# Two feed-forward stages: gate and up products as seven products of quarters, gated values and residual through DRAM, down projection after them

## Chip, cores and metric

The kernel runs on one core of one Trainium2 chip. The metric is the time of one execution on the device in microseconds (us), as the median of several runs. The profile of one execution stands beside it.

## What is computed

Two transformer blocks act on 1024 tokens of width 1024, all in float32, the second on the result of the first. Each has a mixer (attention of several kinds), then a feed-forward part with 2816 hidden features, and it is only this part that the change rewrites:

```python
def hybrid_layer(...):
    ...
    gu = jnp.einsum('bsd,df->bsf', x, w_gu)
    gate, up = gu[..., :FFN_HIDDEN], gu[..., FFN_HIDDEN:]
    ffn = jnp.einsum('bsf,fd->bsd', jax.nn.silu(gate) * up, w_down)
    return layer_norm(DEEPNORM_ALPHA * x + ffn, ln2_g, ln2_b)

def second_block(...):
    ...
    f = (jax.nn.silu(h @ w_gate[l]) * (h @ w_up[l])) @ w_down[l]
    x = x + gate_f * rmsnorm(f, g_ffn_post[l])
```

## The kernel before

**Products.** A float32 product is made of three float32r products. Each operand is split into a high part (rounded to float32r) and a low part (what is left), and TensorE adds high x high, low x high and high x low in one PSUM bank: the lines L444 to L446 (`pe_gemm_f`, features on the bank's partitions) and L469 to L471 (`pe_gemm_t`, tokens on the partitions). All move 512 columns against a 128 x 128 weight block.

**Weights.** A list `plan` names all weight tiles of 512 KB in the order of their use. SyncE loads them into three buffers `raw` (`sp_feed`, L405). ScalarE copies a tile to the high part `wh` (`act_feed`, L416), GpSimd subtracts to get the low part `wl` (`pool_feed`, L425); of each part there are five buffers (`NU = 5`). `ahead(m)` works out how many loads and splits may be issued once unit m is used. In layer 1, tiles of `w_cond_2` ("R" units, the modulation rows of the second block) go through the same three buffers, and VectorE uses them up in `dve_mod` (L1568, L1571).

**Feed-forward part.** The normalised tokens stand transposed and split in `yh`, `yl`. The 22 blocks of 128 hidden features are taken in chunks of 6, 6, 6 and 4. For each feature block and each half of the tokens (512), gate and up take 24 matmuls each. ScalarE takes silu of the gate bank (L1674), VectorE multiplies by the up bank (L1733), ScalarE writes the high part (L1693) and VectorE the low part (L1737) into `hh`, `hl`, which stay in SBUF. After each chunk the down projection of its features is made for 8 blocks of tokens x 2 halves of columns, and VectorE adds each bank into `res` (L1753), which in layer 1 holds the residual, scaled by ScalarE (L1496). Five banks take turns in all of this.

**Order.** Each engine's program is written by hand (`pe_ffn`, `act_ffn`, `pool_ffn`, `dve_ffn`, `sp_ffn`) and run strictly in order; engines wait for each other by semaphores alone. All DMAs are issued from SyncE's queue.

Of the kernel before, what the change touches and what calls it, by code (L numbers as in the profile page):

```python
# [9 lines left out]
F32 = mybir.dt.float32  # L10
# [162 lines left out]
def build(nc, T, out):  # L173
    with ExitStack() as top:
# [37 lines left out]
        x3_out, y_out = sem("x3_stored"), sem("out_stored")  # L212
        xb_in = [sem(f"xb_in{i}") for i in range(4)]
# [58 lines left out]
        def ffn_memory(name):  # L272
            area(upper)
            sil = [sb(f"sil{i}" + name, 512) for i in range(2)]
            hh, hl = [sb("hh" + name, 4096, FR)], [sb("hl" + name, 4096, FR)]
            spare = place[0]
            hh.append(sb("hi" + name, 2048, FR))
            hl.append(sb("hm" + name, 2048, FR))
            return sil, hh, hl, spare

        sil1, hh1, hl1, spare = ffn_memory("_gu")
        macc = [sb(f"macc{i}", 512) for i in range(2)]
        area(spare)
# [14 lines left out]
        sil2, hh2, hl2, spare = ffn_memory("_gate")  # L298

# [19 lines left out]
        ROWS = 6, 5  # L319

        def has_row(a, k, f):
            return a < 18 and f < a + k - 1
# [12 lines left out]
        m = 0  # L335
        for a, k in CHUNKS:
            for f in range(a, a + k):
                plan += [("F", "w_gu", 128 * f), ("F", "w_gu", FF + 128 * f)]
                if has_row(a, k, f):
                    plan += mod_rows(m, 1)  # L340
                    m += 1
            for n in range(2):
                plan += [("T", "w_down", j, 512 * n) for j in range(a // 2, (a + k) // 2)]
                if a < 18:
                    plan += mod_rows(m, ROWS[n])
                    m += ROWS[n]
# [4 lines left out]
        for a, k in CHUNKS:  # L351
            for f in range(a, a + k):
                plan += [("F", "w_gate_2", 128 * f), ("F", "w_up_2", 128 * f)]
            for n in range(2):
                plan += [("T", "w_down_2", j, 512 * n) for j in range(a // 2, (a + k) // 2)]
        unit = {key: m for m, key in enumerate(plan)}
        split_units = [m for m, key in enumerate(plan) if key[0] != "R"]
        split_no = {m: n for n, m in enumerate(split_units)}

        room = {}  # L360

        def ahead(m):

            if m not in room:
# [2185 lines left out]
```

## Time and profile before

| | us |
|---|---|
| median of 3 runs | 2666.53 |
| lowest, highest | 2664.0, 2666.94 |
| the profiled execution | 2664.65 |
| its span | 2662.5 |
| TensorE busy | 2509.5 (94%) |
| VectorE, ScalarE, GpSimd busy | 1144.1, 843.2, 494.5 |
| mean granted TensorE clock | 0.976 of full |
| moved by DMA | 205.44 MB |

The span reaches from the first to the last instruction; what lies around it in the profiled execution is 2664.65 - 2662.5 = 2.15 us. Line numbers (L444) are those of the kernel's file. A matmul's duration in the profile overlaps the next one's, so TensorE's pace is read from the count of matmuls in a stretch and not from their durations.

### The profile page before, as it was taken

How to read it: one execution, taken by the hardware profiler on the slowest of the kernel's cores; microseconds unless marked ns; L12 is line 12 of the kernel's file. 1: busy time of each engine (PE TensorE's matmuls, PEld its weight loads, DVE VectorE, ACT ScalarE, POOL GpSimd, SP SyncE). 2: the span in 40 equal slices, each digit the busy share in tenths (PEclk: the TensorE clock that was granted, in tenths of full speed). 3: DMA queues.
4: the chain of work that ended last, by engine and by line, in shares of the span. 5: the costliest groups of instructions: out<-in, count | busy, mean ns of one | idle time of the engine just before them, and what ended most of it. 6: DMA issues, size and time to landing. Idle time of an engine off the chain costs nothing.

```text
span 2662.5 us, 31098 instructions
## 1 busy us (share of the span) xinstructions
PE 2509.5 (94%) x12551; PEld 2032.0 (76%) x12551; DVE 1144.1 (43%) x2177; ACT 843.2 (32%) x1532; POOL 494.5 (19%) x209
## 2 busy tenths in 40 slices
PE   7999988879999999999999989989899999999998
PEld 6667877668877787787787866667778888888886
DVE  2698897753623223223319037773631111111115
ACT  3556637651311111121123226653421112021112
POOL 2012210001122122222223211021212222222220
PEclk9999988989999999999999999989999999999999
DMA  5015441222033323323412210001411111111122
GB/s 157 16 52 183 161 151 54 101 82 106 8 95 103 95 71 95 96 70 97 151 51 78 78 40 25 17 17 64 135 64 48 40 56 48 52 46 53 57 70 103
DMA packets 195718, 205.44 MB, mean 77 GB/s; under 512 B 13788, under 2 KB 143340, under 8 KB 195576
## 3 DMA queue, kind: packets, MB, share of 16 engines
q1 hardware_dynamic: 195576, 203.46, 24.4%
q8 instruction: 99, 1.62, 0.3%
q14 instruction: 43, 0.35, 0.0%
HBM read 170.88 MB, written 32.56 MB: 76 GB/s over the span
## 4 chain that ended last, share of the span: by engine, by line
PE 77%; DVE 15%; ACT 3%; issue 2%; DMA 2%; POOL 1%; SPq 1%; POOLq 0%; DVEq 0%; ACTq 0%
PE bank L444 15%; PE bank L446 15%; PE bank L445 15%; PE bank L469 8%; PE bank L471 8%; PE bank L470 8%; DVE rest L2136 2%; PE bank L1306 2%; DVE junk L1021 2%; DVE res L1241 1%; POOL wl L425 1%; PE bank L1216 1%; DVE took L2141 1%; PE bank L488 1%; PE bank L1280 1%
## 5 line engine op out<-in xcount | busy, mean ns | idle before, releaser
L425 POOL TENSOR_TENSOR wl<-raw,wh 128x1024 fp32r<-128x1024 f32 x189 | 455.4, 2428 | 2037.9 <-ACT wh L416 2037.9
L444 PE MATMUL bank<-yh,wh 128*128 128x512 f32 x1536 | 602.9, 393 | 5.7 <-ACT sil_gu L1674 2.8
L445 PE MATMUL bank<-yl,wh 128*128 128x512 f32 x1536 | 599.3, 390 | 0.0
L446 PE MATMUL bank<-yh,wl 128*128 128x512 f32 x1536 | 599.3, 390 | 0.0
L416 ACT ACTIVATE wh<-raw 128x1024 fp32r<-128x1024 f32 x189 | 196.1, 1054 | 546.4 <-PE bank L471 242.9
L444 PEld LDWEIGHTS bank<-yh,wh 128*128 128x128 f32 x1536 | 289.7, 189 | 71.9 <-issue 5.4
L446 PEld LDWEIGHTS bank<-yh,wl 128*128 128x128 f32 x1536 | 289.3, 188 | 60.5
L445 PEld LDWEIGHTS bank<-yl,wh 128*128 128x128 f32 x1536 | 289.5, 189 | 59.5 <-issue 0.2
L1733 DVE TENSOR_TENSOR sil_gate<-sil_gate,bank 128x512 f32<-128x512 f32 x44 | 30.3, 688 | 358.9 <-PE bank L446 358.6
L1733 DVE TENSOR_TENSOR sil_gu<-sil_gu,bank 128x512 f32<-128x512 f32 x44 | 30.2, 687 | 324.9 <-PE bank L446 212.0
L1753 DVE TENSOR_TENSOR res<-bank,res 128x512 f32<-128x512 f32 x112 | 76.0, 689 | 214.0 <-PE bank L471 214.0
L469 PE MATMUL bank<-wh,yh 128*128 128x512 f32 x384 | 151.5, 395 | 2.7 <-DVE yl L2153 1.5
L470 PE MATMUL bank<-wl,yh 128*128 128x512 f32 x384 | 149.9, 390 | 0.0
L471 PE MATMUL bank<-wh,yl 128*128 128x512 f32 x384 | 149.8, 390 | 0.0
L1021 DVE TENSOR_SCALAR_CACHE_REDUCE junk<-score,cand 128x384 bf16<-128x384 f32 (+3 forms) x132 | 108.9, 825 | 4.7
L444 PE MATMUL bank<-xh,wh 128*128 128x512 f32 x240 | 96.6, 402 | 6.3 <-POOL wl L425 6.3
L469 PE MATMUL bank<-wh,hh_gu 128*128 128x512 f32 x256 | 100.6, 393 | 1.0 <-POOL wl L425 1.0
L469 PE MATMUL bank<-wh,hh_gate 128*128 128x512 f32 x256 | 99.7, 389 | 1.0 <-POOL wl L425 1.0
L471 PE MATMUL bank<-wh,hl_gu 128*128 128x512 f32 x256 | 99.7, 389 | 0.0
L470 PE MATMUL bank<-wl,hh_gu 128*128 128x512 f32 x256 | 99.6, 389 | 0.0
L471 PE MATMUL bank<-wh,hl_gate 128*128 128x512 f32 x256 | 99.6, 389 | 0.0
L470 PE MATMUL bank<-wl,hh_gate 128*128 128x512 f32 x256 | 99.6, 389 | 0.0
(287 smaller groups left out, 4092.2 us busy)
## 6 DMA issues: line engine op xcount, KB each, us to landing
raw<-in_w_cond SPq DMA_DIRECT2D x48, 512.0 KB, 3.9
raw<-in_w_gu SPq DMA_DIRECT2D x44, 512.0 KB, 5.3
raw<-in_w_down SPq DMA_DIRECT2D x44, 512.0 KB, 3.6
raw<-in_w_in SPq DMA_DIRECT2D x40, 512.0 KB, 4.1
raw<-in_w_gate SPq DMA_DIRECT2D x22, 512.0 KB, 3.9
raw<-in_w_up SPq DMA_DIRECT2D x22, 512.0 KB, 3.9
res<-in_x SPq DMA_DIRECT2D x16, 512.0 KB, 8.4
raw<-in_w_out SPq DMA_DIRECT2D x16, 512.0 KB, 3.6
```

Source lines behind the costliest of these rows:

```text
L416: act.i.activation(wh[n % NU][:, :], raw[u % NRAW][:, :], ACT.Copy).then_inc(*av.up(("wh", u)))
L425: pool.i.tensor_tensor(wl[n % NU][:, :], raw[u % NRAW][:, :], wh[n % NU][:, :].bitcast(F32), ALU.subtract).then_inc(*po.up(("wl", u)))
L444: pe.i.matmul(bank[:, :], a, a_h[:, s], start=k == 0, stop=False)
L445: pe.i.matmul(bank[:, :], a, a_l[:, s], start=False, stop=False)
L446: last = pe.i.matmul(bank[:, :], b, a_h[:, s], start=False, stop=k == 7)
L469: pe.i.matmul(bank[:, 0:wide], xa, h[:, c:c + wide], start=k == 0, stop=False)
L470: pe.i.matmul(bank[:, 0:wide], xa, l[:, c:c + wide], start=False, stop=False)
L471: last = pe.i.matmul(bank[:, 0:wide], xb_, h[:, c:c + wide], start=False, stop=k == nk - 1)
L1021: dve.i.tensor_scalar(junk[:, 0:ln], score[:, o:o + ln], 0.0 if thr is None else thr[:, n:n + 1], 0.0, op, ALU.add, accum_out=cnt[:, n:n + ...
L1306: last = pe.i.matmul(uses.held[t, "out"][:, c0:c1], pt[:, 128 * b:128 * b + 128], v[:, 128 * b + c0:128 * b + c1], start=b == 0, stop=b == i)
L1733: dve.i.tensor_tensor(sil[:, :], sil[:, :], uses.held[key][:, :], ALU.mult).then_inc(*dv.frees(uses, key))
L1753: dve.i.tensor_tensor(dst, uses.held[key][:, :], dst, ALU.add).then_inc(*dv.frees(uses, key))
```

## The change

**Seven products.** The first four feature blocks ("early") of each layer are made as before, 24 matmuls a bank. The other 18 are taken two at a time, gate and up apart: 18 "pairs" q per layer, even q gate, odd q up. A pair is a product of 1024 tokens x 1024 inputs with 256 features. The inputs are cut into quarters (512 tokens x 512 inputs), the weights too (512 inputs x 128 features), and the four quarters of the result are combined from seven products of quarters, in the Winograd form of Strassen's scheme. A product has 4 blocks of inputs x 3 = 12 matmuls, a pair 84 where it had 96.

**Sums of tokens.** Four sums of token quarters are made once per layer while the early features run: VectorE in pieces of 128 x 2048 (`dve_sum`), ScalarE the high part (`act_sum`), VectorE the low part (`dve_sum_low`). `sum1` takes the place of a quarter of `yh`, `yl` that the early features read.

**Differences of weights.** Four differences of 128 x 512 per pair are made by VectorE from the two raw tiles into `res` (`wdiff`, `dve_feed`). The split into high and low is made in pieces of 128 x 512, two to a unit "S".

**Putting together.** ScalarE copies product 0 to SBUF; VectorE makes seven additions with a bank per pair (`dve_pair`); on even pairs ScalarE takes four silus in place, on odd pairs VectorE makes four multiplications.

**Hidden values through DRAM.** Gated values are stored in `qk_d` (22 blocks of 512 KB), read back, and split by ScalarE and VectorE in pieces of 128 x 1024 (`sp_hidden`, `act_hidden`, `dve_hidden`): blocks 0 to 5 beside the last pair, later ones beside the down projection, which is now a stage of its own after all pairs, in the same chunks and with as many matmuls.

**Residual.** In layer 1 the normalised tokens are stored in `x2_d` (`sp_out1`) and read back (`sp_residual`) before the down projection; VectorE scales them in its first addition, and the eight scaling copies of ScalarE (L1496) go.

**Modulation rows.** One row per pair and 5 + 5 per chunk (before 5 in a chunk's features and 6 + 5 in its down part); 48 as before.

```diff
@@ def ffn_plan(layer, m) @@
+            for q in range(N_PAIR):
+                f = N_EARLY + q // 2 * 2
+                units += [("W", wu if q % 2 else wg, (up if q % 2 else 0) + 128 * (f + i)) for i in range(2)]
+                if layer == 1:
+                    units += mod_rows(m, 1)
+                    m += 1
+                units += [("S", layer, i) for i in range((7 * q) // 2, (7 * q + 7) // 2)]
...
+        def operands(u):
+            layer, i = plan[u][1:]
+            out = []
+            for o in (2 * i, 2 * i + 1):
+                b1, b2 = [raw_of(w) for w in pair_units(layer, o // 7)]
+                out.append(((b1[:, 0:512], b1[:, 512:1024], wdiff[1], wdiff[2], wdiff[0], wdiff[3], b2[:, 512:1024])[o % 7],
...
+        def dve_feed(m):
...
+                dve.i.tensor_tensor(t1, b12, b11, ALU.subtract).then_inc(*dv.up())
+                dve.i.tensor_tensor(t3, b22, b12, ALU.subtract).then_inc(*dv.up())
+                dve.wait_ge(*dv.now())
+                dve.i.tensor_tensor(t2, b22, t1, ALU.subtract).then_inc(*dv.up())
+                dve.wait_ge(*dv.now())
+                dve.i.tensor_tensor(t4, b21, t2, ALU.subtract).then_inc(*dv.up(("differences", layer, q)))
...
+                if plan[u][0] == "S":
+                    for k, (src, there) in enumerate(operands(u)):
+                        act.wait_ge(*there)
+                        act.i.activation(wh[n % NU][:, 512 * k:512 * k + 512], src, ACT.Copy).then_inc(*av.up(("wh", u)))
...
+        PRODUCTS = a11, a12, sum2, sum3, sum1, a22, sum4
+        SUM_OF = {2: 2, 3: 3, 4: 1, 6: 4}
...
+        BESIDE_LAST = {1: (0, 1), 3: (2, 3), 5: (4, 5)}
...
+        def pe_pair(layer, q):
+            for s, (high, low) in enumerate(PRODUCTS):
...
+                h, l = pe_unit(u)
+                bank = G["r"].open(key)
+                pe.wait_ge(*G["r"].prior(key))
+                if q == 0 and s in SUM_OF:
+                    pe.wait_ge(*dv.after(("sum_low", layer, SUM_OF[s])))
+                for k in range(4):
+                    c = 512 * (o % 2) + 128 * k
+                    pe.i.matmul(bank[:, :], h[:, c:c + 128], high[:, k, :], start=k == 0, stop=False)
+                    pe.i.matmul(bank[:, :], h[:, c:c + 128], low[:, k, :], start=False, stop=False)
+                    last = pe.i.matmul(bank[:, :], l[:, c:c + 128], high[:, k, :], start=False, stop=k == 3)
...
+        def sp_hidden(layer, f):
+            to, i = landing(f)
...
+            elif f < 6:
+                sp.wait_ge(*dv.after(("landed", layer, f - 2)))
...
+            sp.i.dma_start(to, T["qk_d"][f].rearrange("p (k c) -> p k c", k=2)).then_inc(*hid_in[i].up((layer, f), 16))
...
+        def act_pair(layer, q, s):
+            if s == 0:
...
+                act.i.activation(first[q % 2], uses.held[key][:, :], ACT.Copy).then_inc(*av.frees(uses, key))
+            elif s in ENDS and q % 2 == 0:
+                p = piece(q, *ENDS[s])
+                act.wait_ge(*dv.after(("done", layer, q, s)))
+                act.i.activation(p, p, ACT.Silu).then_inc(*av.up(("gated", layer, q, s)))
...
+                    if not n and not tb:
+                        pe.wait_ge(*dv.after(("landed", layer, a + kk - 1)))
```

**What moves on the engines, by the built programs.** TensorE has 9737 rows where it had 10169: 432 matmuls fewer. The first place is VectorE inside layer 1's pairs. Before, one feature block with its modulation row (`macc`) reads:

```order
L1733 TENSOR_TENSOR sil0_gu_122<-sil0_gu_122,bank0 128x512
L1737 TENSOR_TENSOR hl_gu_125<-sil0_gu_122,hh_gu_124 128x512
L1733 TENSOR_TENSOR sil1_gu_123<-sil1_gu_123,bank2 128x512
L1737 TENSOR_TENSOR hl_gu_125<-sil1_gu_123,hh_gu_124 128x512
L1571 SCALAR_TENSOR_TENSOR macc0_128<-raw2_56,cc_51,macc0_128 128x512 x2
```

Now, at the seam from an odd pair to the even one behind it (the last rows of the odd pair, the differences for the pair after, its row, its first additions):

```order
L1995 TENSOR_TENSOR res_53<-bank4,res_53 128x512
L2002 TENSOR_TENSOR res_53<-res_53 128x512
L477 TENSOR_TENSOR res_53<-raw0_54,raw2_56 128x512
L478 TENSOR_TENSOR res_53<-raw0_54 128x512
L480 TENSOR_TENSOR res_53<-raw0_54,res_53 128x512
L482 TENSOR_TENSOR res_53<-raw2_56,res_53 128x512
L1659 TENSOR_SCALAR macc1_131<-raw1_55,cc_51 128x512
L1662 SCALAR_TENSOR_TENSOR macc1_131<-raw1_55,cc_51,macc1_131 128x512
L1995 TENSOR_TENSOR res_53<-bank1,res_53 128x512
L2006 TENSOR_TENSOR res_53<-bank2,res_53 128x512
```

The differences stand in front of the additions that free the banks, so VectorE waits there for both raw tiles of the next pair. The second place is SyncE's queue in layer 1's pairs. Before, each feature block has this:

```order
L405 DMA raw0_54<-in_w_cond_2 128x2x512 [waits dve_done]
L405 DMA raw1_55<-in_w_gu 128x8x128 [waits pool_done,act_done]
L405 DMA raw2_56<-in_w_gu 128x8x128 [waits pool_done,act_done]
```

Now two pairs have this:

```order
L447 DMA raw1_55<-in_w_cond_2 128x2x512 [waits dve_done]
L447 DMA raw2_56<-in_w_gu 128x8x128 [waits pool_done,act_done]
L447 DMA raw0_54<-in_w_gu 128x8x128 [waits pool_done,act_done]
L2111 DMA qk_d<-res_53 128x1024 [waits dve_done] x2
L447 DMA raw1_55<-in_w_cond_2 128x2x512 [waits dve_done]
L447 DMA raw2_56<-in_w_gu 128x8x128 [waits pool_done,act_done]
L447 DMA raw0_54<-in_w_gu 128x8x128
```

In one pair of two the second tile waits for splits that need the first tile's arrival; in the other both are issued together. Two stores have come in. The third place is SyncE's queue at the end of layer 2's pairs. Before, a chunk's features and its down projection follow on each other with loads of weights alone:

```order
L405 DMA raw2_56<-in_w_gate_2 128x8x128 [waits pool_done,act_done]
L405 DMA raw0_54<-in_w_up_2 128x8x128 [waits pool_done,act_done]
L405 DMA raw1_55<-in_w_gate_2 128x8x128 [waits pool_done,act_done]
L405 DMA raw2_56<-in_w_up_2 128x8x128 [waits pool_done,act_done]
L405 DMA raw0_54<-in_w_down_2 128x2x512 [waits pool_done,act_done]
```

Now:

```order
L1807 DMA res_53<-qk_d 128x1024 [waits early_stored1,early_stored0] x2
L447 DMA raw0_54<-in_w_down_2 128x2x512 [waits pool_done,act_done]
L1807 DMA res_53<-qk_d 128x1024 [waits early_stored1,early_stored0,dve_done] x2
L447 DMA raw1_55<-in_w_down_2 128x2x512 [waits pool_done,act_done]
L1807 DMA res_53<-qk_d 128x1024 [waits hid_stored2,dve_done]
L1807 DMA res_53<-qk_d 128x1024 [waits hid_stored3,dve_done]
```

The six hidden blocks that the first chunk of the down projection needs come in three turns through two landing places, and each of the last four waits for VectorE to have split the block two before it.

## Rows read from the trace of the kernel before

**Rows 1.** Page, busy time by engine; then TensorE clock in 40 slices.

```profile
PE 2509.5 (94%) x12551; PEld 2032.0 (76%) x12551; DVE 1144.1 (43%) x2177; ACT 843.2 (32%) x1532; POOL 494.5 (19%) x209
...
PEclk9999988989999999999999999989999999999999
```

**Rows 2.** Page, chain that ended last, by engine.

```profile
PE 77%; DVE 15%; ACT 3%; issue 2%; DMA 2%; POOL 1%; SPq 1%; POOLq 0%; DVEq 0%; ACTq 0%
```

**Rows 3.** Busy us (x instructions) by stretch, core 0; first line names columns.

```profile
core 0: us, PE busy (x) PEld busy (x) DVE busy (x) ACT busy (x) POOL busy (x), PEclk, DMA share, GB/s
690.00:1440.00 750.00, 743.10 (x3262) 602.54 (x3261) 249.83 (x334) 143.01 (x195) 171.50 (x72) 1.00 0.29 87
...
1940.00:2620.00 680.00, 675.52 (x2976) 559.05 (x2975) 108.64 (x156) 121.50 (x161) 145.16 (x62) 0.99 0.17 52
2100.00:2200.00 100.00, 100.00 (x443) 82.84 (x442) 13.51 (x20) 16.86 (x22) 21.83 (x10) 1.00 0.17 48
```

**Rows 4.** What PE waited for, 690 to 1430 us: total, times, longest.

```profile
PE bank L444 <- ACT sil_gu L1674: 2.8, 1, 2.8
```

**Rows 5.** Groups, 690 to 1430 us: count, busy, mean ns, idle before.

```profile
L425 POOL TENSOR_TENSOR wl<-raw,wh 128x1024 fp32r<-128x1024 f32 x66 | 157.9, 2411 | 588.7 <-ACT wh L416 588.7
...
L1571 DVE SCALAR_TENSOR_TENSOR macc<-raw,cc,macc 128x512 f32<-128x512 f32 x84 | 73.6, 877 | 5.4
L416 ACT ACTIVATE wh<-raw 128x1024 fp32r<-128x1024 f32 x65 | 68.4, 1059 | 313.4 <-DMA raw<-in_w_gu 185.4 <-DMA raw<-in_w_down 107.6 <-PE bank L471 20.3
...
L1737 DVE TENSOR_TENSOR hl_gu<-sil_gu,hh_gu 128x512 fp32r<-128x512 f32 x32 | 31.8, 993 | 22.4 <-ACT hh_gu L1693 22.4
L1733 DVE TENSOR_TENSOR sil_gu<-sil_gu,bank 128x512 f32<-128x512 f32 x44 | 30.2, 687 | 324.9 <-PE bank L446 212.0 <-ACT sil_gu L1674 112.9
...
L1693 ACT ACTIVATE hh_gu<-sil_gu 128x512 fp32r<-128x512 f32 x32 | 20.2, 632 | 136.4 <-DVE sil_gu L1733 136.4
...
L551 DVE SCALAR_TENSOR_TENSOR res<-res,st,b 128x1024 f32<-128x1024 f32 x6 | 7.7, 1284 | 0.2
```

**Rows 6.** GpSimd's two forms of one operation, whole span.

```profile
L688 POOL TENSOR_TENSOR wil<-wir,wih 128x64 fp32r<-128x64 f32 x1 | 0.3, 324 | 4.7 <-ACT wih L677 4.7
```

**Rows 7.** ScalarE in time, 725 to 760 us.

```profile
739.49 1.06 ACT L416 ACTIVATE wh<-raw 128x1024 fp32r<-128x1024 f32 x1 [8.57 <-DMA raw<-in_w_gu]
...
742.12 0.58 ACT L1674 ACTIVATE sil_gu<-bank 128x512 f32<-128x512 f32 x1
```

**Rows 8.** TensorE in time, 736 to 744 us: the gap.

```profile
743.15 0.47 PE L444 MATMUL bank<-yh,wh 128*128 128x512 f32 x1 [2.81 <-ACT sil_gu L1674]
743.45 0.39 PE L445 MATMUL bank<-yl,wh 128*128 128x512 f32 x1
```

**Rows 9.** Loads into raw, 700 to 800 us: issue to landing.

```profile
DMA to landing us min/median/max: 3.8/5.3/7.9
```

**Rows 10.** Page, a DMA issue line: count, KB each, median us to landing.

```profile
raw<-in_w_gate SPq DMA_DIRECT2D x22, 512.0 KB, 3.9
```

**Rows 11.** VectorE in time, 790 to 830 us.

```profile
820.88 0.69 DVE L1733 TENSOR_TENSOR sil_gu<-sil_gu,bank 128x512 f32<-128x512 f32 x1 [8.80 <-PE bank L446]
822.26 2.60 DVE L1737 TENSOR_TENSOR hm_gu<-sil_gu,hi_gu 128x512 fp32r<-128x512 f32 x1 [0.70 <-ACT hi_gu L1693]
```

**Rows 12.** GpSimd in time, same stretch: three instructions end to end.

```profile
817.20 7.12 POOL L425 TENSOR_TENSOR wl<-raw,wh 128x1024 fp32r<-128x1024 f32 x3 [13.92 <-ACT wh L416]
```

**Rows 13.** TensorE in time, 1944 to 1947 us.

```profile
1943.95 1.97 PE L488 MATMUL bank<-con,xb 128*128 128x128 f32 x8 [3.48 <-DVE xb L2308]
...
1946.57 0.63 PE L446 MATMUL bank<-yh,wl 128*128 128x512 f32 x1
```

**Rows 14.** Windows with the columns of rows 3: clock is third from last.

```profile
1944.00:1948.00 4.00, 4.00 (x14) 3.52 (x15) 3.71 (x5) 2.81 (x5) 0.00 (x0) 0.50 0.88 359
1948.00:1952.00 4.00, 4.00 (x16) 3.17 (x15) 1.55 (x3) 1.09 (x2) 0.00 (x0) 0.79 0.00 0
```

More of the change, by code:

```diff
@@ L270, in build @@
         g1, b1 = sb("g1", 1024), sb("b1", 1024)
[L272 to L281, printed above, removed]
+        area(upper)
+        sums = {n: [sb(f"sum{n}{x}", 2048, FR) for x in "hl"] for n in (2, 3, 4)}
+        early = [sb(f"early{i}", 512) for i in range(2)]
         macc = [sb(f"macc{i}", 512) for i in range(2)]
+        wdiff = [res[:, 512 * i:512 * i + 512] for i in range(4)]
+        first, third, whole = [res[:, 2048:2560], res[:, 2560:3072]], res[:, 3072:3584], res[:, 3584:4096]
+        hid = [res[:, 4096:6144], res[:, 6144:8192]]
+        spare = upper + 9216
         area(spare)
@@ L406, in sp_feed @@
                 fed["sp"] += 1
+        def operands(u):
[4 more added lines that the diff above has]
+                out.append(((b1[:, 0:512], b1[:, 512:1024], wdiff[1], wdiff[2], wdiff[0], wdiff[3], b2[:, 512:1024])[o % 7],
+                            loaded(pair_units(layer, o // 7)[o % 7 > 1]) if o % 7 in (0, 1, 6) else dv.after(("differences", layer, o // 7))))
+            return out
@@ new lines, in next_hidden, with blocks_of, hidden_store, piece @@
+        def next_hidden(a, n, tb):
+            i = 8 * n + tb
+            last = min(a + 12, 22)
+            return a + 6 + i // 2 if a < 18 and i % 2 and a + 6 + i // 2 < last else None
+        BESIDE_LAST = {1: (0, 1), 3: (2, 3), 5: (4, 5)}
+        def blocks_of(q):
+            f = N_EARLY + q // 2 * 2
+            return f, hid[(f // 2 + 1) % 2]
+        def hidden_store(f):
+            return 2 * ((f // 2 + 1) % 2) + f % 2
+        def piece(q, block, half):
+            c = 1024 * block + 512 * half
+            return blocks_of(q)[1][:, c:c + 512]
@@ L1718, in pool_ffn, with dve_pair @@
                         after_block(tb)
+        def dve_pair(layer, q, s):
+            if s == 0:
+                return
+            key = ("product", layer, q, s)
+            bank, u, f = uses.held[key], first[q % 2], blocks_of(q)[0]
+            dve.wait_ge(*mm.after(key))
+            dve.wait_ge(*dv.now())
+            if s in ENDS:
+                to = whole
+                if q % 2 == 0:
+                    to = piece(q, *ENDS[s])
+                    for i in range(2):
+                        dve.wait_ge(*hid_out[hidden_store(f + i)].after((layer, f + i - 4)))
+                if s == 1:
+                    dve.wait_ge(*av.after(("product", layer, q, 0)))
+                dve.i.tensor_tensor(to, bank[:, :], third if s in (4, 5) else u, ALU.add
+                                    ).then_inc(*(dv.up() if s == 4 else dv.frees(uses, key)))
+                dv.also(("done", layer, q, s))
+                if q % 2:
+                    p = piece(q, *ENDS[s])
+                    dve.wait_ge(*av.after(("gated", layer, q - 1, s)))
+                    dve.wait_ge(*dv.now())
+                    dve.i.tensor_tensor(p, whole, p, ALU.mult).then_inc(*dv.up(("hidden", layer, q, s)))
+            if s == 3:
+                dve.i.tensor_tensor(third, bank[:, :], u, ALU.add).then_inc(*dv.frees(uses, key))
+            elif s in (2, 4):
+                dve.i.tensor_tensor(u, bank[:, :], u, ALU.add).then_inc(*dv.frees(uses, key))
```

518 lines of the change are left out of this document (363 added, 155 removed).

## The prediction

> **What bounds the kernel now.** I read the page first. TensorE is busy for 94% of the span at nearly full clock, no other engine for half of it [rows 1], and the chain of waits that ended last lies on TensorE for 77% [rows 2]. Then the table by stretch: both feed-forward stages, 690 to 1440 us and 1940 to 2620 us, are TensorE without gaps, 743.10 of 750 and 675.52 of 680 us, while VectorE has 249.83 and 108.64 us of work there and GpSimd 171.50 and 145.16 [rows 3]. In layer 1 TensorE waited for another engine's result hardly at all; the one long wait is 2.8 us [rows 4]. So a matmul taken out here is worth its whole pace, as long as the other engines keep up. That pace is read from a stretch with nothing else in it: 443 matmuls in 100 us, 0.2257 us each [rows 3].
>
> **What goes.** Per layer 18 pairs with 84 matmuls instead of 96, so 2 x 18 x 12 = 432, as the built programs also show (10169 rows, now 9737). 432 x 0.2257 = **97.5 us**. The down projection and the early features keep their matmuls. A product now takes 12 x 0.2257 = 2.71 us, a pair 19.0 us. The 2.8 us wait comes from a bank whose silu stood behind ScalarE's splits, which waited for late loads [rows 4, 7, 8]; those loads were held up by the modulation row in front of them, and since the first features run in another order now and the next loads have another place, I take this wait as gone: 2.8 us. The scaling copies of ScalarE are off TensorE's path and count nothing either way.
>
> **What comes, engine by engine.** The work of a pair of 19.0 us in layer 1:
> - VectorE: 4 differences, 7 additions, 2 multiplications (4 in every second pair), 2 row updates. A 128 x 512 operation takes 0.69 us [rows 5, 11], a row update 0.88 us [rows 5]: 13 x 0.69 + 1.8 = 10.8 us.
> - ScalarE: 7 half splits at 0.63, a copy at 0.6, on average 2 silus at 0.58 [rows 5, 7]: 6.2 us.
> - GpSimd: 7 half subtractions. No row has 128 x 512. Between 0.32 us for 64 columns [rows 6] and 2.41 us for 1024 [rows 5] a straight line gives 1.3 us, the upper bound is 2.41 (as if a half cost as much as a whole). I take 1.3, since 64 columns cost so little: 9.1 us; at the bound it would be 16.9 us, still under 19.0.
> - DMA: 22 stores and 22 loads of 512 KB more per layer and the residual there and back, on DMA engines that are busy for 29% and 17% of these stretches [rows 3]; the weights are as many as before.
>
> None of them is the bound by its sum. What can cost is order. Four places:
>
> *1. The start of layer 1's pairs.* The sums run on VectorE beside the early features (4 x 96 x 0.2257 = 87 us). A piece of 128 x 2048 isn't in the trace; from 0.69 us for 512 and 1.28 for 1024 columns [rows 5] I extend to 2.4 us (bounds 1.28 and 2.8). Fourteen of them are 34 us, covered. But `sum1` may be written only when the last early product has ended, and product 4 of pair 0 needs it 4 x 2.71 = 10.8 us later. In between lie, in layer 1, the second raw tile of pair 1 (its buffer comes free late, 4 to 5 us), four differences (2.8), ScalarE's half split and high part (0.6 + 1.9, extended in the same way) and VectorE's low part (2.4): 12 to 13 us. With a lock or two as in case 2, I take 3 us lost, with 0 and 8 as ends. In layer 2 the buffers have no modulation rows in them and the tile is early: 0.
>
> *2. Raw buffers in layer 1's pairs.* The three buffers hold two tiles of a pair and a modulation row, and the next tile may come only when the last piece of the old one is split. Over two pairs the chain is: load 3.9 (one alone [rows 9, 10]), ScalarE and GpSimd half 1.9, load 3.9, differences 2.8, half split 0.6, row update with first addition and silu 2.8 and split 1.3, four GpSimd halves 5.2; then two loads together 5.2, differences 2.8, half split 0.6, four halves 5.2. Sum 36.2 us, against 2 x 19.0 = 37.9 us of matmuls (unrounded). To this comes a wait that the trace shows: a VectorE operation with both inputs in SBUF took 2.60 us instead of 0.69 [rows 11], because GpSimd was at work from 817.20 for 7.12 us, three instructions end to end [rows 12], and VectorE's result came 0.54 us after these had ended. The operation just before, with one input in PSUM, took 0.69. GpSimd will be busy for 9.1 of 19.0 us, so each of some ten such operations in the chain waits 0.48 x 0.65 = 0.3 us on average: 3.1 us. The chain is then 39.3 us, 1.4 us longer than the matmuls, nine times in layer 1: 12.6 us, of which the splits that run ten products ahead hide some 8. I take **5 us**, between 0 and 33. In layer 2 two tiles share three buffers and the same chain is near 28 us: 0.
>
> *3. From the pairs to the down projection, both layers.* Counted from the start of the last pair, TensorE is done at 19.0. Hidden blocks 0 and 1 are loaded by then, but their places are free only after product 1, at 5.4. ScalarE takes 1.06 [rows 5], VectorE 1.28 (its one form of 1024 columns in the stage, L551) [rows 5]: block 0 split at 7.8, block 1 at 9.4. Each turn from there is a load (3.9 alone [rows 10], 4.1 with another behind it), 1.06 and 1.28, so 6.4 us: block 3 at 15.8, block 5 at 22.2, and with 1.3 us for the waits of case 2, 23.5. TensorE waits 4.5 us. After such a gap its clock is low: when it had waited 3.48 us [rows 13] the granted clock was 0.50 for the next 4 us, its level of 1.2 GHz, and 0.79 in the 4 us after [rows 14], and a matmul lasted 0.63 us [rows 13]; but after the 2.81 us gap the next one had 0.39 at once, as everywhere at full clock [rows 8]. Some 5 us at half pace lose about 2 us; I take these. Together 6.5 us per layer, **13 us**; ends 0 and 22.
>
> *4. Layer 1's first chunk.* The residual's last blocks, hidden blocks 6 to 9 and modulation rows queue behind the store of block 21. VectorE then frees its first bank some 3 us late and stands at hidden block 6 until about 15 us into the chunk; five banks of 4.1 us cover that. The last weight tile of the second half is there about when it is needed. I take 1 us, ends 0 and 6.
>
> **The sum.** 2664.65 - 97.5 - 2.8 + 3 + 5 + 13 + 1 = 2586.4 us for the profiled execution. That one lies 1.9 us under the median of 2666.53, so as a median **2588 us**, 2.9% faster.
>
> **A rule against this change.** The rows show that VectorE waited for GpSimd, once. The Trainium skill ("SBUF — State Buffer", Who interferes with whom) is stricter: GpSimd and a VectorE instruction with two SBUF inputs hold the shared port pair for a whole instruction, and the other one "fully blocks". The change puts six to eight such instructions into each pair and cuts GpSimd's work into pieces, so by that rule nearly every one may meet a lock; what that would give is the fourth case below. For the sums the skill has a figure too ("GPSIMD Engine Reference", Elementwise side-by-side cycle accounting): 2293 ns for 128 x 2048 on VectorE, which would take 0.1 us off each piece and leave the sum as it is.
>
> **Cases.**
> - *Forecast, 0.48:* 2575 to 2600 us.
> - *All covered, 0.15:* loads land in 3.8 us and the hidden blocks make it: 2666.5 - 97.5 - 2.8 + 2 = 2568 us. For it: TensorE hardly waited in either stage before [rows 4]. Against it: three turns of 6.4 us don't fit into 13.6 us.
> - *Layer 1's raw buffers become the bound, 0.30:* loads of w_gu take 5.3 us in the median and up to 7.9 [rows 9], and ScalarE stood 8.57 us before one [rows 7]. With 1.4 us more for each of three load steps the chain is 39.3 + 4.2 = 43.5 us, 5.6 more than the matmuls, nine times: 50 - 8 = 42 instead of 5, so 2625 us; half of the excess gives 2604. Against it: these 5.3 us are of loads issued three at a time, and the same kind alone lands in 3.9 [rows 10].
> - *Slower than before, 0.04:* the shared port locks at every meeting. Place: layer 1's chain of case 2. Ten VectorE operations wait a whole 1.3 us each instead of 0.3 and GpSimd halves cost 2.41 instead of 1.3 (nine of them in the chain): 43.5 + 10 + 10 = 63.5 us, 25.6 over, nine times 230 - 8: 2588 - 5 + 222 = 2805 us. It decides from the point where the chain passes 37.9 + (2666.5 - 2588 + 5 + 8) / 9 = 48 us. Against it: 9.1 of 19.0 us is GpSimd's share, not all.
> - *Something that I can't place, 0.03,* of either sign.
>
> That the change doesn't do what it says is excluded by the count of rows.
>
> **Range and chances.** A measurement of this kernel tells about 0.2% (5.3 us) from no change. 2569 us takes in most of the second case, 2622 us most of the third. Faster 0.95, within 0.2% 0.01, slower 0.04.
>
> **What will show it.** The stage of layer 1 is shorter by about 36 us (48.8 + 2.8 - 3 - 5 - 6.5 - 1) and that of layer 2 by 42 (48.8 - 6.5). TensorE's waits show one of 4 to 5 us before the first matmul of the down projection, for VectorE's low part of block 5, with a granted clock near 0.5 behind it in both layers; one of a few us for VectorE's `yl` at product 4 of layer 1's first pair; and in layer 1's pairs few or none. If the pairs of layer 1 take over 19.5 us and those of layer 2 19.0, the raw buffers bind. GpSimd's 128 x 512 pieces near 1.3 us, VectorE's differences at 0.69 with some up to 2.0. I am wrong if layer 2's pairs have waits, if TensorE's pace in a product isn't 0.2257 us, or if the early features take more than 87 us.

## Result and profile after: 2619.28 us

| | before | after |
|---|---|---|
| median | 2666.61 (4 runs) | 2619.28 (4 runs, 2619.0 to 2620.41) |
| the profiled execution | 2664.65 | 2619.53 |
| its span | 2662.5 | 2617.4 |

The ratio is 0.9825 (95% 0.9808 to 0.9842): 47 us, or 1.8%, faster, where 78 us were forecast. The time lies inside the range, near its slow end.

The page's busy time and granted clock by slice, and the chain of waits by engine, against [rows 1, 2]:

```profile
PE 2427.5 (93%) x12119; PEld 1959.3 (75%) x12119; DVE 1517.2 (58%) x2557; ACT 931.6 (36%) x1704; POOL 677.5 (26%) x389
...
PEclk9999988889999999999999999998989999999999
...
PE 61%; DVE 19%; DMA 7%; POOL 5%; ACT 4%; issue 3%; SPq 1%; DVEq 0%; POOLq 0%; ACTq 0%
```

TensorE has 432 matmuls fewer and is still the busiest. But the chain now lies on it for 61% and no longer for 77%; DMA has come to 7% of it and GpSimd to 5%. Where, a table by stretch tells (columns of [rows 3]): the stage of layer 1 with the start of the next mixer, layer 1's 18 pairs, and those of layer 2.

```profile
691.62:1531.57 839.95, 797.84 (x3453) 642.41 (x3451) 465.97 (x573) 209.56 (x328) 289.30 (x173) 0.98 0.36 120
782.20:1157.10 374.90, 358.23 (x1521) 289.30 (x1519) 219.67 (x269) 104.44 (x180) 168.64 (x121) 0.97 0.34 108
2013.00:2356.00 343.00, 342.94 (x1513) 283.62 (x1512) 178.80 (x231) 109.62 (x181) 164.55 (x122) 1.00 0.29 91
```

The first stretch, from the first early product to the first matmul of the next mixer, was this long before:

```profile
692.96:1538.15 845.19, 833.71 (x3669) 676.67 (x3667) 279.46 (x383) 169.23 (x243) 196.16 (x83) 1.00 0.29 86
```

So layer 1 gained 5.2 us where 36 were forecast. Layer 2's stage begins 4.8 us ahead (1939.17 against 1943.95 us) and ends 45.1 ahead: 40.3 gained where 42 were forecast. In layer 2's pairs TensorE works without a gap, 19.05 us each, as predicted; in layer 1 the same 18 pairs take 32 us more (4 of them are the modulation rows' own short matmuls, which the prediction's 19.0 us per pair left out: without a wait these pairs take 347.4 us, e1 below). Here is what TensorE waited for, 690 to 1445 us, where [rows 4] had one wait:

```profile
PE bank L1855 <- ACT res L1916: 16.4, 6, 4.5
PE bank L558 <- DVE res L2063: 11.0, 4, 7.9
PE bank L558 <- DVE sum3l L1820: 6.7, 1, 6.7
...
PE bank L1855 <- DVE yl L1768: 0.2, 1, 0.2
```

Three places, then: inside the pairs (16.4 us), at the handover to the down projection (6.7), and in the last chunk of the down projection (11.0). The last row is the wait for `sum1`, for which 3 us had been set aside. In layer 2, 1935 to 2610 us, the handover comes again:

```profile
PE bank L558 <- DVE sum3l L1820: 6.4, 1, 6.4
```

**One stall in the pairs**, 861 to 878 us in time (start, duration, instruction, idle before):

```profile
861.85 7.68 SPq L447 DMA_DIRECT2D raw<-in_w_gu  x2
...
865.78 1.16 ACT L495 ACTIVATE wh<-raw 128x512 fp32r<-128x512 f32 x2 [8.11 <-DMA raw<-in_w_gu]
866.55 2.54 POOL L510 TENSOR_TENSOR wl<-raw,wh 128x512 fp32r<-128x512 f32 x2 [4.78 <-ACT wh L495]
...
873.79 0.69 DVE L477 TENSOR_TENSOR res<-raw,raw 128x512 f32<-128x512 f32 x1 [9.53 <-DMA raw<-in_w_gu]
...
876.57 0.63 ACT L495 ACTIVATE wh<-res 128x512 fp32r<-128x512 f32 x1 [9.63 <-DVE res L482]
...
877.11 0.58 ACT L1916 ACTIVATE res<-bank 128x512 f32<-128x512 f32 x1
```

SyncE issues the first tile of the next pair at 861.85 us. It lands 3.9 us later; ScalarE makes two high halves, GpSimd two low halves, done at 869.09. Only then is the second tile issued (the two issues, 7.68 us with the wait between them, end at 869.53), and it lands at 873.8. VectorE's four differences and ScalarE's half split stand in front of the copy of product 0 (L1916), and that copy frees the bank for which TensorE waits:

```profile
877.74 0.79 PE L1855 MATMUL bank<-yh,wh 128*128 128x512 f32 x1 [4.49 <-ACT res L1916]
878.33 0.63 PE L1856 MATMUL bank<-yl,wh 128*128 128x512 f32 x1
```

Matmuls then stand 0.43 us apart instead of 0.2267 until 883.8 us, for 6 us, at the lower of the two clocks, 1.2 GHz: the granted clock (third from last) was 0.50 behind this wait and 0.51 behind the one at layer 2's handover.

```profile
877.70:881.70 4.00, 3.96 (x9) 3.13 (x10) 3.39 (x6) 3.16 (x6) 3.80 (x4) 0.50 0.43 135
2362.30:2368.70 6.40, 6.36 (x15) 5.00 (x16) 2.64 (x2) 0.00 (x0) 2.22 (x1) 0.51 0.44 143
```

How long is the chain over two pairs? The first of the four differences is made 17 times in layer 1's pairs, so from the first to the last there are eight periods of two pairs. Line L477, 780 to 1165 us:

```profile
L477 DVE TENSOR_TENSOR res<-raw,raw x17: 691/693/1687, 785.2 to 1125.7; 128x512 f32<-128x512 f32 x17
...
  DMA raw<-in_w_gu: 94.1, 14
```

(1125.7 - 785.2) / 8 = **42.6 us**, and before 14 of the 17 VectorE stood idle for a tile, 94 us in all. Predicted were 39.3.

**The last chunk of layer 1.** VectorE before the change and after it:

```profile
1314.85 0.21 DVE L1596 TENSOR_TENSOR macc<-macc 128x48 f32<-128x48 f32 x1 [10.44 <-DMA macc<-in_b_cond]
1324.79 1.23 DVE L1802 SCALAR_TENSOR_TENSOR gp<-sh,gp 128x1024 f32<-128x1024 f32 x1 [9.73 <-DMA sh<-vec_d]
```

```profile
1381.17 0.21 DVE L1687 TENSOR_TENSOR macc<-macc 128x48 f32<-128x48 f32 x1 [9.26 <-DMA macc<-in_b_cond]
1391.04 1.23 DVE L2153 SCALAR_TENSOR_TENSOR gp<-sh,gp 128x1024 f32<-128x1024 f32 x1 [9.66 <-DMA sh<-vec_d]
1392.18 1.28 DVE L2063 TENSOR_TENSOR res<-bank,res 128x512 f32<-128x512 f32 x2
```

The same two waits of VectorE, 19 to 20 us, stood there before. TensorE then had four feature blocks in front of it (4 x 96 x 0.2257 = 87 us) whose first banks it needed back late; now the chunk is down projection alone, a bank fills in 2.7 us, five are full after 13.6, and TensorE stands for 7.9 us.

### The profile page after: what moved, and what is told of

Its sections match the earlier page's. It is cut to its first block, busy times and chain, and to the rows that moved or that the text cites. A ratio compares the mean times of both kernels' runs of the same rounds, so it can differ in the third digit from the quotient of the medians.

```text
span 2617.4 us, 31377 instructions
## 1 busy us (share of the span) xinstructions
PE 2427.5 (93%) x12119; PEld 1959.3 (75%) x12119; DVE 1517.2 (58%) x2557; ACT 931.6 (36%) x1704; POOL 677.5 (26%) x389
## 4 chain that ended last, share of the span: by engine, by line
PE 61%; DVE 19%; DMA 7%; POOL 5%; ACT 4%; issue 3%; SPq 1%; DVEq 0%; POOLq 0%; ACTq 0%
PE bank L558 8%; PE bank L560 8%; PE bank L559 8%; PE bank L534 5%; PE bank L535 5%; PE bank L536 5%; PE bank L1855 5%; PE bank L1857 5%; PE bank L1856 5%; DMA raw<-in_w_gu 4%; POOL wl L510 4%; DVE rest L2487 2%; PE bank L1395 2%; DVE junk L1110 2%; DVE res L1330 1%
## 5 line engine op out<-in xcount | busy, mean ns | idle before, releaser
L515 POOL TENSOR_TENSOR wl<-raw,wh 128x1024 fp32r<-128x1024 f32 x117 | 294.0, 2527 | 1390.0 <-ACT wh L498 1390.0
L558 PE MATMUL bank<-wh,yh 128*128 128x512 f32 x768 | 303.7, 395 | 28.0 <-DVE sum3l L1820 13.1
L560 PE MATMUL bank<-wh,yl 128*128 128x512 f32 x768 | 300.5, 391 | 0.0
L1855 PE MATMUL bank<-yh,wh 128*128 128x512 f32 x576 | 228.6, 397 | 16.7 <-ACT res L1916 16.4
L510 POOL TENSOR_TENSOR wl<-raw,wh 128x512 fp32r<-128x512 f32 x108 | 155.1, 1450 | 283.0 <-ACT wh L495 283.0
L1857 PE MATMUL bank<-yh,wl 128*128 128x512 f32 x576 | 227.2, 395 | 0.0
L1856 PE MATMUL bank<-yl,wh 128*128 128x512 f32 x576 | 227.2, 394 | 0.0
L510 POOL TENSOR_TENSOR wl<-res,wh 128x512 fp32r<-128x512 f32 x144 | 191.3, 1351 | 119.5 <-ACT wh L495 99.2
L534 PE MATMUL bank<-yh,wh 128*128 128x512 f32 x384 | 154.0, 401 | 2.9 <-DVE ql L2383 1.4
L535 PE MATMUL bank<-yl,wh 128*128 128x512 f32 x384 | 151.1, 393 | 0.0
L536 PE MATMUL bank<-yh,wl 128*128 128x512 f32 x384 | 150.9, 393 | 0.0
L1855 PEld LDWEIGHTS bank<-yh,wh 128*128 128x128 f32 x576 | 109.8, 191 | 45.7 <-ACT res L1916 19.0
L1857 PEld LDWEIGHTS bank<-yh,wl 128*128 128x128 f32 x576 | 109.9, 191 | 23.2
```

What stands on the lines that cost most here:

```text
L510: pool.i.tensor_tensor(wl[n % NU][:, half], src, wh[n % NU][:, half].bitcast(F32), ALU.subtract).then_inc(*po.up(("wl", u)))
L515: pool.i.tensor_tensor(wl[n % NU][:, :], raw_of(u)[:, :], wh[n % NU][:, :].bitcast(F32), ALU.subtract).then_inc(*po.up(("wl", u)))
L534: pe.i.matmul(bank[:, :], a, a_h[:, s], start=k == 0, stop=False)
L535: pe.i.matmul(bank[:, :], a, a_l[:, s], start=False, stop=False)
L536: last = pe.i.matmul(bank[:, :], b, a_h[:, s], start=False, stop=k == 7)
L558: pe.i.matmul(bank[:, 0:wide], xa, h[:, c:c + wide], start=k == 0, stop=False)
```

## Experiments

"The changed kernel" on a run's chip is 0.9825 x the kernel before there: 2618.1 us for the first four runs, 2617.2 and 2620.0 for the later ones. An interval of a ratio is about 3.5 us to either side; that of the changed kernel's own ratio is 4.5 us, so a difference to it below 5 us or so is not told from nothing.

### Half pieces (e1_half_keys)

```diff
-                        pool.wait_ge(*av.after(("wh", u)))
+                        pool.wait_ge(*av.after(("wh", u, k)))
...
-                        sp.wait_ge(*av.after(("wh", last_split(before))))
-                        sp.wait_ge(*po.after(("wl", last_split(before))))
+                        k = last_half(before)
+                        sp.wait_ge(*av.after(("wh", last_split(before), k)))
+                        sp.wait_ge(*po.after(("wl", last_split(before), k)))
```

> The edit: GpSimd's half piece waits for ScalarE's half piece alone instead of the whole unit, and a raw buffer of a pair is released by the half piece that reads it last instead of the whole unit. No instruction more or less. Theory A, the chain through the raw buffers of layer 1's pairs is too long (in the changed kernel the pairs of layer 1 take 374.9 us where those of layer 2 take 343, and in one stall the second tile was issued at 869.1 us, only after the first had landed at 865.8 and been split): the second tile can be issued with the first, one load of 4 us leaves a chain of 42 us per two pairs, which is then about 38, the matmuls' own 37.9. TensorE's waits for res at L1916, 16.4 us in six, fall under 3 us and the time by 20 to 30 us, to 2590 to 2600. Theory B, TensorE's waits come from where ScalarE's copy and VectorE's additions stand behind the next pair's splits and differences, whatever the loads do: the waits stay in number, shrink by a microsecond each, and the time falls by less than 8 us.

Measured: **2591.34 us**, ratio 0.9722 (0.9708 to 0.9735), 27 us under the changed kernel. The stretch of the pairs (their first matmul starts at 784.41 us here, and they end at 1131.85), then the same difference (it is L485 here):

```profile
784.41:1131.85 347.44, 347.44 (x1521) 283.67 (x1519) 216.94 (x272) 109.71 (x181) 167.79 (x121) 1.00 0.37 117
```

```profile
L485 DVE TENSOR_TENSOR res<-raw,raw x17: 678/680/1333, 785.8 to 1095.3; 128x512 f32<-128x512 f32 x17
...
  DMA raw<-in_w_gu: 2.1, 2
```

No wait is left in layer 1's pairs, the period is (1095.3 - 785.8) / 8 = 38.7 us, and VectorE's idle time for tiles has gone from 94 to 2 us. Theory A holds. The pairs had lost 374.9 - 347.4, **some 27 us**: 16.4 of waits, about 9 of lower clock behind the four long ones, and the rest at the edges of the waits, where the matmuls' spacing is 0.2 to 0.3 us longer than the wait's row says.

### Half of that edit (e8_pool_half)

Only the first line of the diff above: GpSimd waits for its own half, the buffers stay with the whole unit.

> Of the edit of the first run only one half: GpSimd's half piece waits for ScalarE's half piece alone, while a raw buffer is still released by the whole unit. Theory A, what costs the time is that the release of the buffer for the second tile waits for the first tile's arrival (the whole unit holds the last half of the old pair and the first half of the next): only 0.6 us per stall is saved, 2612 to 2617 us. Rival B, it is GpSimd's late start that made the chain long: most of the 28 us come back, 2592 to 2600 us.

Measured: **2595.55 us**, ratio 0.9747 (0.9734 to 0.9761), 21.6 under the changed kernel. Rival B's number came, and theory A's 0.6 us per stall was wrong. GpSimd and SyncE of this kernel:

```profile
851.00 5.50 POOL L511 TENSOR_TENSOR wl<-res,wh 128x512 fp32r<-128x512 f32 x4 [2.81 <-DVE res L1996]
856.47 1.75 POOL L511 TENSOR_TENSOR wl<-raw,wh 128x512 fp32r<-128x512 f32 x1
861.39 2.54 POOL L511 TENSOR_TENSOR wl<-raw,wh 128x512 fp32r<-128x512 f32 x2 [3.17 <-ACT wh L495]
```

```profile
856.58 6.54 SPq L447 DMA_DIRECT2D raw<-in_w_gu  x2
```

The second tile still waits for the first (6.54 us for two issues). But GpSimd now does the old pair's last half (856.47) while the first tile is on its way. In the changed kernel it had idled there from 861.8 to 866.6 us, because it waited for the high part of a whole unit, whose other half is of the next tile. That puts 1.2 us less between landing and second issue (2.1 instead of 3.3). Each row of low halves also starts 0.8 us after the high parts begin instead of 1.3, twice per period. That is 2.2 us of the 3.1 by which the period, 784.6 to 1100.2 in eight, went down, from 42.6 to 39.4. With 0.7 over the matmuls' 38.7 left and splits running ahead, the pairs hardly waited (one of 0.3 us). So the chain was the cause, and its longest avoidable part was GpSimd's late start, not the order of the two loads. The loads' share is what lies between this run and the last, 4 to 6 us, little more than the two intervals allow; the traces have it at the handover of layer 1, where TensorE waited 8.3 us here and 4.3 in e1's kernel.

### Place instead of length (e2_feed_later)

```diff
-                    if (7 * q + s) % 2:
+                    if (7 * q + s) % 2 and not (layer == 1 and s == 6 and q < N_PAIR - 1):
                         act_feed(operand_unit(layer, 7 * q + s))
```

and the same for `dve_feed`.

> The edit: in layer 1, what ScalarE and VectorE do for the next operands behind an odd pair's last product (half splits, and the four differences) is put behind the next pair's product 1, so the copy of product 0 and the additions that free the banks stand in front of it. Theory A, the chain of loads, differences and splits is longer than the matmuls (42 against 37.9 us per two pairs): the banks come free in time, but the same microseconds are then missed as waits for wh or wl, and the later place costs as much as it gives: within 5 us of 2619, or slower by up to 20. Theory B, the place alone costs the time: the six waits for res go and nothing comes in their stead, 2592 to 2600 us.

Measured: **2614.63 us**, ratio 0.981 (0.9796 to 0.9823), 3.5 less, inside theory A's 5 and not to be told from nothing. The period is still (1120.6 - 786.6) / 8 = 41.8 us. TensorE's waits, 690 to 1445 us:

```profile
PE bank L558 <- DVE sum3l L1820: 12.6, 1, 12.6
PE bank L558 <- DVE res L2063: 11.0, 4, 8.2
PE bank L1855 <- DVE res L1995: 6.1, 4, 2.1
PE bank L1855 <- ACT res L1916: 1.7, 3, 0.7
```

The waits for the copy fell from 16.4 to 1.7 us, but 6.1 came for the additions, and the last pair's lateness came out at the handover, 12.6 instead of 6.7. Freeing a bank sooner does not shorten a chain. They did not come as waits for `wh` or `wl`, as theory A had put it.

### Why layer 1 and not layer 2 (e10_rows_down, e11_all_rows_down)

```diff
-        ROWS = 5, 5
+        ROWS = 8, 8
...
-                if layer == 1:
-                    units += mod_rows(m, 1)
-                    m += 1
```

and no row in the pairs of the three engines' programs.

> The changed kernel, with all 48 modulation rows beside the down projection (eight per half of a chunk instead of five) and none beside the pairs of layer 1, whose three raw buffers then hold two tiles each pair as in layer 2; the waits for half pieces and for buffers stay as they are. Theory A, layer 1's pairs are late because the third buffer holds a modulation row, so that each tile's load waits for the splits of the pair before (42.6 us from one difference to the next but one, where the first run's edit gave 38.7): the six waits for res (16.4 us) and the half clock behind them vanish, the pairs take 343 us as in layer 2, and the time is 2590 to 2597 us if the down projection hides 18 more rows (1.76 us of VectorE each, 32 us in 202). Rival B, the unit-wise waits of GpSimd bind by themselves (the run before gave most of the time back by these alone): waits stay in layer 1's pairs, over 2605 us. Rival C, the down projection becomes bound by rows and weights in turn through three buffers: its waits grow by 10 us or more, over 2600.

Measured: **2656.51 us**, ratio 0.9958 (0.9944 to 0.9971), 36.5 more than the changed kernel. Both A's mechanism and C came true, each in its stage:

```profile
L474 DVE TENSOR_TENSOR res<-raw,raw x17: 681/685/1345, 786.0 to 1091.3; 128x512 f32<-128x512 f32 x17
```

```profile
PE bank L555 <- POOL wl L512: 37.6, 17, 3.6
```

The period is (1091.3 - 786.0) / 8 = 38.2 us and the pairs have no wait, with GpSimd's waits as they were. So it takes both, the third buffer's row and GpSimd's whole-unit wait, to make the chain too long. Rival B's size (over 2605) is met, but not for its reason. In the down projection five rows per half leave room for the weights, and eight do not: TensorE waits 17 times for a low part of `w_down` (once, for 0.2 us, in the changed kernel's), and a granted clock of 0.92 from 1134 to 1429 us (0.98 in the changed kernel) adds to it.

> The same on top of the kernel with all three edits (2575.7 us). If the rows beside the pairs cost nothing once the half pieces are there, it is 2571 to 2579 us, no change; if some of their locks and queueing still cost, 2565 to 2570.

Measured: **2642.54 us**, ratio 0.991 (0.9897 to 0.9924). Neither range: on top of the three edits of the sections below, the rows in the down projection cost 66 us more than beside the pairs. This run's expectation had stood on A alone.

### The handover (e3_four_places, e7_split_place)

```diff
+            if f in (2, 3):
+                return hid[0][:, 1024 * (f % 2):1024 * (f % 2) + 1024].rearrange("p (k c) -> p k c", k=2), 4 + f
...
-        BESIDE_LAST = {1: (0, 1), 3: (2, 3), 5: (4, 5)}
+        BESIDE_LAST = {1: (0, 1), 2: (2, 3), 4: (4, 5)}
```

SyncE's program has the loads of blocks 0 to 3 together at product 0 now, and those of 4 and 5 at product 2. (e7: the last key is 3, and e1's edit is in it.)

> The edit: hidden blocks 2 and 3 of the first chunk get landing places of their own, so the six blocks come in two turns beside the last pair and not in three. Theory A, TensorE waits 6.74 and 6.40 us at the first matmul of each down projection because each of the three turns is a load, a high part and a low part one after the other: both waits go, and with them the 2 us or so of half clock behind each, 13 to 17 us in all, 2602 to 2606 us. Rival B, the waits are for VectorE's and GpSimd's work as such (both share these microseconds with the last splits) and not for the turns: each wait shrinks by 2 us at most and the time is over 2612.

Measured: 2615.85 us (2613.36 to 2621.02), ratio 0.9815 (0.98 to 0.983): 2 us less, within the interval. The waits at the handovers fell to 2.85 and 3.73 us, so A and B are each half right. The 6.6 us won there are not in the time: the profile is of the slowest of the five runs (2621.02 us), and in it the pairs of layer 1 waited 18.7 us for the copy instead of 16.4, and `wl` took 3.1 instead of 1.4 us. Whether the edit does that isn't shown. Layer 2's handover, VectorE, GpSimd and TensorE:

```profile
2360.12 4.49 DVE L1825 TENSOR_TENSOR sum3l<-res,sum3h 128x1024 fp32r<-128x1024 f32 x2
```

```profile
2360.48 6.37 POOL L515 TENSOR_TENSOR wl<-raw,wh 128x1024 fp32r<-128x1024 f32 x2 [1.43 <-ACT wh L498]
```

```profile
2364.67 0.50 PE L558 MATMUL bank<-wh,yh 128*128 128x512 f32 x1 [3.73 <-DVE sum3l L1825]
```

VectorE had block 4's high part from 2358.1 us and began at 2360.12, behind additions; then it and GpSimd held each other up, 4.49 us instead of 2.5 and 6.37 instead of 4.8. That leaves two causes of 2 us each, and the next run moves the one that a line can move.

> On top of the first run's edit (2591.3 us, with waits of 4.3 and 6.5 us at the two handovers): four landing places as in the run before, and VectorE's low parts of hidden blocks 4 and 5 stand behind product 3 of the last pair instead of product 4. Theory A, what was left of the wait with four places (2.85 and 3.73 us) was the place in VectorE's order: high part ready at 2358.1, low part begun at 2360.12 us behind four additions: both waits fall under 1.5 us, no half clock behind them, 2579 to 2583 us. Rival B, it was GpSimd: its two whole subtractions from 2360.48 us took 6.37 us where two take 4.8, and VectorE's two low parts 4.49 where two take 2.5, each in the other's way: the waits stay near 3 us, 2584 to 2588 us.

Measured: **2578.65 us**, ratio 0.9683 (0.967 to 0.9696), 11 under e1's kernel on this chip (0.9722 x 2663.78 = 2589.7). Theory A:

```profile
PE bank L568 <- DVE sum3l L1835: 1.1, 1, 1.1
```

That, in layer 2, is the only such wait left; in layer 1 a wait of 1.7 us for a modulation row took its place. GpSimd's overlap cost VectorE 0.6 us here (two low parts in 3.10). The earlier place took the low parts out of GpSimd's way as well, so the run shows that the place is enough, but does not part the two causes.

### The last chunk (e4_gain_later, e6_rows_early)

```diff
-                if a == 18:
+                if a == 18 and layer == 2:
                     before_last()
...
                     if a == 18 and n == 1:
+                        if layer == 1 and tb == 1:
+                            before_last()
                         after_block(tb)
```

> The edit: in layer 1 VectorE's multiplication by the scale row, which waits for a load that follows another load (9.66 us idle to 1391.04 us), is moved from in front of the last chunk's additions to behind its second block of tokens; the row has a semaphore of its own. Theory A, TensorE's wait of 7.9 us at 1392.92 and the smaller ones behind it (1.3, 1.6, 1.2 us) come because VectorE stands there while five banks fill in 5 times 2.7 us: they go, with some 2 us of half clock, and the time falls by 8 to 12 us, to 2607 to 2611. Rival B, VectorE is late already by the wait before it (9.26 us idle to 1381.17 us for the last modulation row): then the 7.9 us only shrink to about 4, and the time falls by 3 to 5 us.

Measured: 2616.39 us, ratio 0.9817 (0.9803 to 0.983): 1.7 less, below either theory and not to be told from nothing. VectorE began its additions at 1380.94 instead of 1392.18 us, and stood again. TensorE's waits for `res` fell from 11.0 to 6.7 us, but the clock went low behind two of them and no longer behind one:

```profile
1380.94 1.28 DVE L2064 TENSOR_TENSOR res<-bank,res 128x512 f32<-128x512 f32 x2
...
1389.34 1.28 DVE L638 SCALAR_TENSOR_TENSOR res<-res,st,g 128x1024 f32<-128x1024 f32 x1 [5.37 <-DMA gp<-in_g_mix_pre]
```

The norm's gain `g` is loaded in the same queue, behind the store of the modulation vector, so the wait moved by one step. Hence the next edit, on SyncE's queue (with e1's edit in it):

```diff
+            sp.wait_ge(*mm.after(("down", 1, 12, 1, 7)))
+            for t, src in ((g2, T["ln2_g"]), (b2, T["ln2_b"]), (gp, T["g_mix_pre_2"])):
+                sp.i.dma_start(t[:, :], src.partition_broadcast(128)).then_inc(*ln2_in.up("ln2", 16))
+            sp_feed(u)
             sp.wait_ge(*dv.after("mod_whole"))
```

> On top of the first run's edit (2591.3 us): the norm vectors' loads and the last modulation row's store and reload are issued in front of the weights for the next mixer, VectorE's last row addition stands behind the first block of tokens of the last chunk and the multiplication by the scale row behind the second. Theory A, in the last chunk of layer 1's down projection VectorE starts 15 us late because of two loads behind one another (first addition at 1392.2 us in the changed kernel, its bank ready at 1376.5), and TensorE's waits there (7.7, 1.2, 0.4, 1.6 us and 1.7 us of half clock) all come from this: they go but for some 2 us, and the time is 2579 to 2583 us. Rival B, VectorE needs 7.0 us for each block of tokens there and TensorE 5.4, so VectorE is the bound of this chunk whatever its start: the waits move to the later blocks and less than 5 us are won, 2586 to 2590.

Measured: **2582.3 us**, ratio 0.9695 (0.9682 to 0.9708), 7.4 under e1's kernel. The time is in A's range, but its account is not: 5.4 us of waits for `res` are left, where 2 were expected.

```profile
PE bank L569 <- DVE res L2078: 5.4, 3, 3.6
```

VectorE's first addition of the chunk is at 1345.08 us, as soon as its bank is full. But a block of tokens takes 7.0 us of VectorE and 5.4 of TensorE (24 x 0.2257), so TensorE runs into VectorE anyway, later: B's mechanism. It is not alone: in the same chunk VectorE stood 3.5 and 3.2 us for two of these loads (to 1352.59 and 1357.73 us), and no run parts the two.

### All three (e9_all)

> All three edits together: half pieces, four places with the earlier low parts, rows early. If the three losses are at three places and independent (28 in the pairs of layer 1, some 10 at the handovers, some 10 in the last chunk of layer 1), it is 2568 to 2574 us; if they hide one another, it stays above 2578.

Measured: **2575.69 us** (2571.23 to 2577.2), ratio 0.9664 (0.9651 to 0.9677): 88 us under the kernel before and 42 under the changed one. The time lies between the two ranges expected. Of 7.4 + 11 = 18 us over e1, 14 came; the shortfall of 4 is within the intervals.

## Why the prediction was off, by its own steps

- **Matmuls removed, 97.5 us, and the old wait, 2.8:** right. Layer 2's pairs take 19.05 us each without a gap and its stage gained 40.3 us of 48.8, with the handover as its only loss. The pace was 343.00 / 1513 = 0.2267 us, 0.4% over the 0.2257 forecast.
- **Engines by their sums:** right. A GpSimd half took 1.29 us undisturbed (forecast 1.3), and no engine reached TensorE's time in a pair.
- **Case 2, raw buffers in layer 1's pairs: the step that failed.** Forecast 5 us, found 27. The mechanism and the place were named rightly: a ring through the raw buffers, longer than the matmuls. Its size was wrong. The chain of 39.3 us measured 42.6. In the two seams that I followed, four terms were too small. From a first tile's arrival to the next issue it was 3.3 us instead of 1.9, as GpSimd waits for both high halves, which stands in the code. The second tile took 4.7 instead of 3.9. Two tiles issued together took 7.0 instead of 5.2 (844.42 to 851.41 us). GpSimd started 1.3 us behind ScalarE instead of 0.6. That is 4.7 us more. The locks, for which 3.1 had been added, were in part in these. Why the loads took longer than forecast is open. The matmuls of two pairs, with those of the rows, take 38.7 us and not 37.9. So (42.6 - 38.7) x 9 = 35 us, less 27, is 8 hidden, as assumed. The rest of the failure is the choice among ends: with chain and matmuls 1.4 us apart, each error of 1 us counts nine times, and the likeliest single value should not have stood at the kind end.
- **The third case** (2625 us, chance 0.30), which set the slow end of the range, is the nearest to 2619, but in part by luck. Its reason was loads 1.4 us slower in each of three steps, 4.2 us in all; the loads gave 0.8 + 1.8, and the other 2.1 came from GpSimd's waits for whole units, which no case named and whose removal alone gave 21.6 us (e8). And it had 42 us for the pairs and nothing for the last chunk, two errors that nearly cancel.
- **Case 3, the handover:** forecast 13 us for both layers, found 6.7 + 6.4 of waits and some 4.5 of clock (8 and 15 matmuls at the wider spacing). The three turns were half of it: two turns alone left 2.85 and 3.73 us (e3), two turns with an earlier place 1.1 (e7). In the recorded sum block 1 stands at 9.4 us, where its own terms give 9.1; that changes nothing here.
- **Case 1, `sum1`:** forecast 3, found 0.2. Splits ahead covered it.
- **Case 4, the first chunk:** forecast 1, found 0.2.
- **Missing altogether: the last chunk of layer 1**, some 14 us by the spacing of its matmuls: 11.0 of waits, the rest at their edges and in the clock. Layer 1's losses are 51.6 - 5.2 = 46.4 us; the pairs' 27, the handover's 8.5, the 0.4 for `sum1` and these 14 are 50. The 3 to 4 us too many are mostly old waits that no step had counted: TensorE waited four times, 2.5 us, for `wl` in layer 1's down projection before, and once for 0.2 us now. The change took away four feature blocks that had covered two waits of VectorE, 20 us in the profile before. The prediction asked what the down projection waits for at its start and never at its end.
- **The port lock**, the rule of the Trainium skill ("SBUF — State Buffer", Who interferes with whom), weighed as a rival with 0.04: the trace agrees with the rule, but the meetings were few. In layer 1's pairs VectorE made 104 differences and additions with both inputs in SBUF (L477 to L482, L2002). The 25 that began while GpSimd was at work all lasted longer, 0.71 to 1.79 us, and the other 79 took 0.68 to 0.69. That is three meetings in two pairs, where the rival had ten. The first differences (L477) took 693 ns in the median and 1687 at most, and the additions (L2002) 948 ns in the mean, 0.26 over 0.69, near the 0.3 assumed.

Besides the pairs, the handover and the last chunk there are some 2 us that the next mixer lost (6.6 us ahead at its start, 4.8 at its end); no run here shows why.

## To carry to other kernels

When a load may be issued only after a split of an earlier load, write the ring of waits out as a period and compare it with the period of the matmuls. Read each wait in it from the semaphore's key and not from the data that it needs: here a key for two halves, where one would do, cost 21 us. When work is taken out of a stage, or moved to another, go through the waits of the other engines in the profile before and ask which of them that work had been covering.

## What was not expected of the hardware

A wait of 2.15 us was followed by three matmuls at full pace, and then by 3.5 us at half. TensorE, e4's kernel:

```profile
1402.15 0.50 PE L559 MATMUL bank<-wh,yh 128*128 128x512 f32 x1 [2.15 <-DVE res L2064]
1402.49 0.39 PE L560 MATMUL bank<-wl,yh 128*128 128x512 f32 x1
...
1403.22 0.63 PE L560 MATMUL bank<-wl,yh 128*128 128x512 f32 x1
```

The clock was back at 1406.6 us. Ten microseconds before, TensorE had waited 2.68 us and run at half pace at once (matmuls 0.43 us apart from 1393.11 to 1396.1 us), while before the change a gap of 2.81 us had cost no clock [rows 8]. So the length of a gap by itself does not tell whether the clock falls. Nor does it set the price: behind the seven gaps of 2.79 to 7.90 us in the two stages of the changed kernel 8 to 15 matmuls stood 0.43 us apart, which cost 1.3 to 2.9 us, least behind the longest gap and most behind those of 4.49 and 6.40 us.

VectorE and GpSimd both lost where they met, as in e3's rows above: two operations each of 128x1024, 2.0 us more on VectorE and 1.6 on GpSimd.
